# The four mLSTM heads: next head's projections and output gates as chunks inside a head's chain

## The reference

```python
u = rms_norm(x) @ w_in_odd        # q, k, v, o of 4 heads x 256, and input and forget gates
k = k / 16;  o = sigmoid(o)       # per head
# log forget gates summed along the tokens, a running maximum m as stabiliser,
# weights w[t, s] = exp(gate_s - m_t) for s <= t
# prompt:  h = ((q k^T) * w) v / max(|den|, exp(-m)),  den = row sums of (q k^T) * w
# samples: C = decay * C + inp * k v^T,  n likewise,  h = C q / max(|n q|, exp(-m))
y = x + concat_heads(head_norm(h) * o) @ w_out_odd
```

## Time and profile before

| | us |
|---|---|
| median of 3 runs | 3177.26 (3173.38 to 3179.24) |
| the profiled execution | 3176.19 |
| its span, first to last instruction | 3174.5 |
| PE, DVE, ACT busy in the span | 2564.2, 1857.0, 958.3 |
| granted TensorE clock, mean of the span | 0.881 of 2.4 GHz |
| the four heads, first L2382 copy to the last `head_over` | 1550.3 to 1921.0 |

### The profile page before, as it was taken

One profiled execution on the slowest core, in us unless ns is written; L12 is line 12 of the kernel. 1 busy time (PEld: TensorE's weight loads), 2 busy tenths in 40 slices (PEclk: granted clock), 3 DMA queues, 4 the chain that ended last, 5 costly groups with the idle time before them and its releaser, 6 DMA issues. The chain is left out here.

```text
span 3174.5 us, 44526 instructions
## 1 busy us (share of the span) xinstructions
PE 2564.2 (81%) x17937; PEld 1897.6 (60%) x17937; DVE 1857.0 (58%) x2161; ACT 958.3 (30%) x1339; POOL 179.1 (6%) x268
## 2 busy tenths in 40 slices
PE   5967887777867899997877777868569999999992
PEld 4755665276652688885666555744445665665662
DVE  4366785395331545435556654322459989989983
ACT  2102231001220100002221221200258878878861
POOL 1130000310100000000000000000100000000001
PEclk8977888757878899998989888879789999999995
DMA  4564223431505122122122112114279999999973
GB/s 149 139 190 168 87 99 108 133 116 54 212 0 199 67 107 107 72 83 107 57 107 110 57 73 90 54 53 186 71 275 384 388 377 387 385 380 387 386 284 87
DMA packets 156880, 537.70 MB, mean 169 GB/s; under 512 B 15787, under 2 KB 51543, under 8 KB 149057
## 3 DMA queue, kind: packets, MB, share of 16 engines
q1 hardware_dynamic: 122018, 439.46, 36.9%
q0 software_dynamic: 18528, 85.75, 8.0%
q10 hardware_dynamic: 16128, 9.64, 1.1%
HBM read 501.55 MB, written 45.80 MB: 172 GB/s over the span
## 5 line engine op out<-in xcount | busy, mean ns | idle before, releaser
L720 PE MATMUL scalar_unit<-arena,weight_parts 128*128 128x260 bf16 (+1 forms) x4032 | 481.8, 282 | 81.1 <-DVE arena L1807 67.3
L720 PEld LDWEIGHTS scalar_unit<-arena,weight_parts 128*128 128x128 f16 (+1 forms) x4032 | 400.1, 100 | 160.0 <-issue 45.7
L720 PE MATMUL vector_unit<-arena,weight_parts 128*128 128x260 bf16 (+1 forms) x3936 | 451.6, 277 | 40.2 <-DVEq L2216 18.6
L720 PEld LDWEIGHTS vector_unit<-arena,weight_parts 128*128 128x128 f16 (+1 forms) x3936 | 388.8, 99 | 98.2 <-DVEq L2216 18.7
L1282 PE MATMUL vector_unit<-weight_parts,arena 128*128 128x512 bf16 (+3 forms) x1536 | 318.9, 364 | 3.7 <-PE scalar_unit L1244 3.0
L1282 PEld LDWEIGHTS vector_unit<-weight_parts,arena 128*128 128x128 f16 (+1 forms) x1536 | 148.3, 98 | 150.7 <-issue 8.0
L2639 DVE SCALAR_TENSOR_TENSOR weight_parts<-stream_ring,weight_parts 128x2048 f16<-128x2048 f32 (+2 forms) x108 | 204.8, 1940 | 21.6 <-ACT weight_parts L1666 21.3
L2639 DVE SCALAR_TENSOR_TENSOR weight_parts<-arena,weight_parts 128x2048 f16<-128x2048 f32 (+2 forms) x106 | 196.5, 1896 | 27.4 <-ACT weight_parts L1666 27.4
L1756 DVE TENSOR_TENSOR weight_parts<-stream_ring,weight_parts 128x4096 bf16<-128x4096 f32 (+3 forms) x45 | 184.2, 4094 | 1.5
L1666 ACT ACTIVATE weight_parts<-stream_ring 128x2048 bf16<-128x2048 f32 (+2 forms) x108 | 170.6, 1631 | 10.6 <-PE scalar_unit L1282 10.1
L1325 ACT ACTIVATE squares<-residual 128x520 f32<-128x520 f32 x56 | 35.7, 637 | 457.3 <-DVEq L1818 402.3
(11 more groups left out here) (477 smaller groups left out, 3424.0 us busy)
## 6 DMA issues: line engine op xcount, KB each, us to landing
stream_ring<-in_expert_w_gu SPq DMA_DIRECT2D x80, 1024.0 KB, 9.6
arena<-in_expert_w_gu SPq DMA_DIRECT2D x80, 1024.0 KB, 9.3
arena<-in_expert_w_dn SPq DMA_DIRECT2D x64, 704.0 KB, 8.3
stream_ring<-in_expert_w_dn SPq DMA_DIRECT2D x64, 704.0 KB, 8.4
stream_ring<-in_mem_kv SPq DMA_DIRECT2D x16, 2048.0 KB, 7.7
stream_ring<-in_ffn_w_gu SPq DMA_DIRECT2D x11, 2048.0 KB, 7.9
stream_ring<-in_xattn_wkv SPq DMA_DIRECT2D x8, 2048.0 KB, 7.9
stream_ring<-in_w_in_odd SPq DMA_DIRECT2D x8, 2048.0 KB, 8.6
```

Of the source, the lines that this page charges most:

```text
L720: ins = mm(u[0:cols, a * 512:a * 512 + w], weight if i else weight.bitcast(F16), x.bitcast(F16) if j else x, start=(k == 0 and i + j == 0) ...
```

## The change

Queries and keys get two buffers, used by heads in turn (`HQS`, `HKS`). The second pair lies over the first four rows of FM: so the rows that are needed in all heads move to rows 4 and 5, and the samples' gate columns go to a small tile FS. PE gets `head_chunk(c)`, which runs one chunk of 48 matmuls and posts `parts_free` itself after each fourth. Chunks 0 to 5 (q, k, v) of head 0 run before the loop. Inside a head, chunks 6 and 7 (the head's own output gates) stand behind the second and the fourth block of scores; chunks 0 to 5 of the next head stand behind the second key half, the first and the second query half, the sum for the sample denominators, and (two) the sum of squares. ACT reads each of them at matching places: the output gates behind the exponentials, queries and keys behind the state, values behind the square root, and posts `head_ready` after these. DVE splits the load with chunks 0 to 3 of the next head at a head's start and the load with its chunks 4 to 7 behind the gate work, ahead of the copies to HH.

The diff, with renamings and blank lines left out; the remarks behind # are added here:

```diff
-    HQ = at(4160, 2, T)
-    HK = at(5200, 2, T)
+    HQS = [at(4160, 2, T), at(14480, 2, T)]
+    HKS = [at(5200, 2, T), at(15520, 2, T)]
+    FS = at(24040, 2, NB, rows=4)
...
+        def head_chunk(c):
+            if c % 4 == 0:
+                pe.wait_ge(sem("parts_ready"), due("parts_ready"))
+                parts_used[0] += 1
+            wt = parts[:, (parts_used[0] - 1) % 2].rearrange("p t (c k m) -> p t c k m", c=4, k=DC)
+            pe.wait_ge(sem("scalar_unit_free"), due("scalar_unit_free"))
+            u = take_unit["scalar"]()
+            for a in range(2):
+                for k in range(DC):
+                    for i, j in ((0, 0), (0, 1), (1, 0)):
...
+            ins.then_inc(sem("scalar_unit_ready"), 1)
+            if c % 4 == 3:
+                pe.wait_ge(sem("scalar_unit_ready"), due("scalar_unit_free", 0))
+                pe.sem_inc(sem("parts_free"), 1)
+        for c in range(6):
+            head_chunk(c)
         for h in range(NH):
-            project(H, 8, DC, 4, ["scalar"] * 8)
+            HQ, HK, last = HQS[h % 2], HKS[h % 2], h == NH - 1
...
                 ins.then_inc(sem("vector_unit_ready"), 1)      # after a block of scores
+                if sb_ % 2:
+                    head_chunk(6 + sb_ // 2)
...
                     ins.then_inc(sem("vector_unit_ready"), 1)  # after a half of L1178
+                    if not last and (src is HQ or half):
+                        head_chunk(0 if src is HK else 1 + half)
...
             ins.then_inc(sem("vector_unit_ready"), 1)          # after L1185
+            if not last:
+                head_chunk(3)
             pe.wait_ge(sem("head_out"), due("head_out"))
             over_features(sq, 2, "vector")
+            if not last:
+                head_chunk(4)
+                head_chunk(5)
...
+        read_queries(0)
+        read_values()
         for h in range(NH):                                    # ACT
-            if h:
-                act.wait_ge(sem("head_over"), due("head_over"))
-            for i, dst in enumerate((HQ, HK, HV, HO)):
...
             act.wait_ge(sem("w_exp"), sent("w_exp"))
+            if h:
+                act.wait_ge(sem("head_over"), due("head_over"))
+            for c in range(2):
+                read_chunk(HO[:, c, :], ACT.Sigmoid)
             act.wait_ge(sem("c_in"), 16 * (h + 1))
...
                 act.sem_inc(sem("c_prompt_done"), 1)
+            if h + 1 < NH:
+                read_queries(h + 1)
             act.wait_ge(sem("head_h"), due("head_h"))
...
             act.wait_ge(sem("root"), sent("root"))
+            if h + 1 < NH:
+                read_values()
+                act.sem_inc(sem("head_ready"), 1)
...
+        for i in range(2):                                     # DVE, gate part
+            V.tensor_copy(FS[:, i, :], FM[0:4, i, S:T]).then_inc(sem("vector_steps"), 1)
...
         dve.sem_inc(sem("gate_rows"), 1)
+        split_weights()
         for h in range(NH):
-            split_weights()
             split_weights()
...
             dve.wait_ge(sem("w_exp"), due("w_exp"))
+            if h + 1 < NH:
+                split_weights()
             for part in range(2):                              # copies to HH
```

More of the change, by code:

```diff
@@ L1114, in _ @@
         project(H, 1, DC, 1, ["scalar"], cols=64, wait_chunks="normed")
+        def head_chunk(c):
[8 more added lines that the diff above has]
+                    for i, j in ((0, 0), (0, 1), (1, 0)):
+                        weight, x = wt[:, i, c % 4, k, :], H[:, j, k, a * HT:a * HT + HT]
+                        ins = mm(u[:, a * 512:a * 512 + HT], weight if i else weight.bitcast(F16), x.bitcast(F16) if j else x,
+                                 start=(k == 0 and i + j == 0), stop=(k == DC - 1 and i == 1))
+            ins.then_inc(sem("scalar_unit_ready"), 1)
[4 more added lines that the diff above has]
+            head_chunk(c)
         for h in range(NH):
-            project(H, 8, DC, 4, ["scalar"] * 8)
+            HQ, HK, last = HQS[h % 2], HKS[h % 2], h == NH - 1
             if h == 0:
@@ L1134, in _ @@
             u = take_unit["vector"]()
-            mm(u[:, 0:S], pick[:, h, :], FM[0:4, 3, 0:S], start=True, stop=True)
-            mm(u[:, S:S + NB], pick[:, h, :], FM[0:4, 0, S:T], start=True, stop=True)
-            ins = mm(u[:, S + NB:S + 2 * NB], pick[:, h, :], FM[0:4, 1, S:T], start=True, stop=True)
+            mm(u[:, 0:S], pick[:, h, :], FM[0:4, 4, 0:S], start=True, stop=True)
+            mm(u[:, S:S + NB], pick[:, h, :], FS[:, 0, :], start=True, stop=True)
+            ins = mm(u[:, S + NB:S + 2 * NB], pick[:, h, :], FS[:, 1, :], start=True, stop=True)
             ins.then_inc(sem("vector_unit_ready"), 1)
@@ L1581, in _, with read_chunk, read_queries, read_values @@
         act.wait_ge(sem("gate_arg"), due("gate_arg"))
-        A(FM[0:4, 4, :], FM[0:4, 3, :], ACT.Ln).then_inc(sem("gate_value"), 1)
+        A(FM[0:4, 3, :], FM[0:4, 4, :], ACT.Ln).then_inc(sem("gate_value"), 1)
         act.wait_ge(sem("gate_value"), sent("gate_value"))
         act.wait_ge(sem("gate_arg"), due("gate_arg"))
-        A(FM[0:4, 5, 0:S], FM[0:4, 4, 0:S], ACT.Exp, scale=-1.0).then_inc(sem("gate_value"), 1)
+        A(FM[0:4, 5, 0:S], FM[0:4, 3, 0:S], ACT.Exp, scale=-1.0).then_inc(sem("gate_value"), 1)
         act.wait_ge(sem("gate_value"), sent("gate_value"))
-        for h in range(NH):
-            if h:
-                act.wait_ge(sem("head_over"), due("head_over"))
-            for i, dst in enumerate((HQ, HK, HV, HO)):
[L1592 to L1597, removed]
+        def read_chunk(dst, fn=ACT.Copy, factor=1.0):
+            act.wait_ge(sem("scalar_unit_ready"), due("scalar_unit_ready"))
+            u = next_unit()
+            A(split(dst), halves(u), fn, scale=factor).then_inc(sem("scalar_unit_free"), 1)
+            act.wait_ge(sem("scalar_unit_free"), sent("scalar_unit_free"))
+        def read_queries(h):
+            for c in range(2):
+                read_chunk(HQS[h % 2][:, c, :])
+            for c in range(2):
+                read_chunk(HKS[h % 2][:, c, :], factor=0.0625)
+        def read_values():
+            for c in range(2):
+                read_chunk(HV[:, c, :])
+        read_queries(0)
+        read_values()
+        for h in range(NH):
             if h == 0:
@@ L1603, in _ @@
                 act.sem_inc(sem("gc_ready"), 1)
-            act.sem_inc(sem("head_ready"), 1)
+                act.sem_inc(sem("head_ready"), 1)
             for dst in (KTOK, VTK):
@@ L2329, in _ @@
         dve.wait_ge(sem("gates_raw"), due("gates_raw"))
-        ig, lf, e_, u_, l_, x_ = (FM[0:4, i, :] for i in range(6))
+        ig, lf, e_, u_, l_, x_ = (FM[0:4, i, :] for i in (0, 1, 2, 4, 3, 5))
         V.tensor_scalar(u_, lf, -1.0, None, ALU.mult).then_inc(sem("vector_steps"), 1)
@@ L2366, in _ @@
         dve.wait_ge(sem("vector_steps"), sent("vector_steps"))
+        for i in range(2):
+            V.tensor_copy(FS[:, i, :], FM[0:4, i, S:T]).then_inc(sem("vector_steps"), 1)
+            dve.wait_ge(sem("vector_steps"), sent("vector_steps"))
         V.tensor_copy(MMP[0:4, 0:1], l_[:, S - 1:S]).then_inc(sem("vector_steps"), 1)
@@ L2372, in _ @@
         dve.sem_inc(sem("gate_rows"), 1)
+        split_weights()
         for h in range(NH):
-            split_weights()
+            HQ, HK = HQS[h % 2], HKS[h % 2]
             split_weights()
```

## The result

The changed kernel takes 3123.9 us (median of 4 runs, 3119.1 to 3129.9) against 3176.7 for the kernel before on the same chip: a ratio of 0.983, with an interval of 0.982 to 0.985. The forecast was 3122. The profiled execution took 3124.8, its span is 3123.1.

What follows compares the result with a forecast made beforehand. No engine was full: each head ran dense projection chunks, then DVE's chain, in series. Three heads -46.8, entry -10.1 and last head +2.2 gave -54.7 us, from 3177.26 to 3122 us, range 3110 to 3151.

Steps and rivals of the forecast that it cites:

- the last head: Last head: no split and no next head, but chunks 6 and 7 stand in it: 2.2 us more.
- 1, wait for score block 2 (L2452): Scores: chunk 6 stands ahead of score block 2, ready at tau 8.85 where DVE wanted it at 7.73: +1.2 us.
- step 2: Weight split moved into mid-chain, ahead of DVE copies that the third product needs: +5.9 us, including the scores' 1.2.
- 3, waits for the query halves: States: the next head's chunks 0 and 1 delay the two query halves: +2.45 and +2.35 us.
- step 4: Norm: chunk 3 and ACT's read stand before the squares, +3.6 us; sums take 1.9 instead of 3.42, -1.5.
- step 5: To the next head: DVE's other split comes last, next copy at tau 84.4; PE's work has 3.9 us of cover.
- The clock: Lower clock after two PE pauses of over 3 us, before the third product and score block 1: 2 us a head.
- Rival (a): Clock falls at both pauses, slowing the whole f32 block and chunk 6: 11.5 us a head, 3151 us; chance 0.20.
- The sentence on the Trainium skill: Bursts after pauses start cold, transposes don't count as activity: chunk 6 cold in every head, 3131 us; possible only.
- The entry: Before the first chain: six chunks stand there instead of eight, 10.1 us less.
- (b): Chunks stay at the half clock, cut up by waits: a head about 140 us, the kernel 3290 us; chance 0.05.
- (c): Chunk 3 or 5 waits for a split held up behind DVE's chain: heads near 102 us, kernel 3167 to 3177; chance 0.05.

Runs made afterwards that it cites:

- e1: Changed kernel with the mid-chain weight split moved to where DVE waits for the sums of squares: 3103.4 us, 0.978 of the kernel before.
- e3: Changed kernel with the next head's chunks 0 to 3 put back behind the chain, after the sums of squares: 3158.6 us, 0.994 of the kernel before.
- e6: Changed kernel with ACT's squares put ahead of its read of chunk 3: 3122.9 us, 0.983 of the kernel before.
- e2: Changed kernel with the mid-chain split moved to DVE's wait for the sums, and the head-start split put in mid-chain: 3114.2 us, 0.981 of the kernel before.
- e5: Changed kernel with 12 unused f32 matmuls filling each of PE's two pauses of over 3 us: 3117.6 us, 0.981 of the kernel before.
- e8: Changed kernel with the mid-chain split moved to DVE's wait for the sums, and the head-start split in three pieces in the chain: 3102.1 us, 0.976 of before.
- e4: Changed kernel with chunks 6 and 7 (output gates) put back ahead of the chain: 3156.0 us, 0.994 of the kernel before.

## Why the prediction was right

The sum for the stage was -54.7 and the stage fell by 54.7, but two errors cancel: the three heads gave 48.0 instead of 46.8, and the last head lost 3.5 instead of 2.2. That the total agrees to a tenth is luck; the terms agree to about 1.3. By step, for head 1, in tau from the copy at 1633.01:

| step | predicted | measured |
|---|---|---|
| 1, wait for score block 2 (L2452) | 1.2 | 1.1 (2.8 in the last head, behind a slow chunk 6) |
| 2, split in mid-chain | 15.1 to 21.9 | 15.0 to 21.7 |
| 2, L2489 | 25.05 | 26.8 |
| 3, L2520 | 33.3 | 35.1 |
| 3, waits for the query halves | 2.45, 2.35 | 2.39, 2.09 |
| 4, sums of squares | 1.9 long | 2.02 long |
| 4, L2565 | 65.7 | 66.8 |
| 5, PE's row ready | 80.5 | 81.5 |
| 5, next copy | 84.4, with the clock 86.4 | 85.7 |

**Steps 1 to 5** hold in kind, and but for the clock to about 0.4 us in size; e1 (step 2), e3 (steps 3 and 4), e6 (step 4) and e2 (step 5) each undid one, and each moved the stage the way of its step. The 1.75 us by which L2489 is late is the clock: the third product takes 4.11 us, and 2.42 in e5. Some of it is made up again further on, for L2565 is only 1.1 late. In step 4, e6 puts the read ahead of the squares at 1.8 us.

**The clock** was put at 2 us a head outside the steps, for either of two pauses. Both pauses stood where the prediction had them (3.28 us before the third product, 3.17 before the score block), and e5 prices them at 1.1 to 1.7 a head. So this term was about 0.6 too large, which covers the 0.4 a head that came beyond the forecast. Rival (a) had the clock fall at both pauses and take the f32 block with it; in the kernel after only one is hit in a head, and behind the third product the f32 block is back at its pace (1.12 and 3.72 us for row and state in head 1). As its sign the prediction named a granted clock of 1.00 around tau 20 to 30 and at chunk 6, and 0.5 as that of (a). By this sign the forecast did not come out clean: the clock is 0.57 at the third product of head 1 and 0.70 and 0.86 at the score block and chunk 6 of head 2. What sets it apart from (a) is the size, 1.4 us a head by e5 against 11.5.

The sentence on the Trainium skill (TensorE: Matmul & The Clock Gate, section HAM oscillation, and Part 4) would have chunk 6 cold, at the lower clock, in every head. Head 0 has no pause ahead of its chunk 6 (5.48 us). In heads 1 to 3, with the same transposes and the same 3.17 us pause ahead of it, chunk 6 takes 5.48, 7.10 and 6.78 us: in one of three it isn't cold, and in the other two it loses 1.6 and 1.3 us and not the 4.9 that the prediction charged. So here the measurement decides against the rule as the prediction applied it.

**The last head** is the term that was mis-sized: +2.2 forecast, +3.5 measured. The prediction charged the clock to three heads only, but the fourth copy has the same pause behind it. These are the score block and chunk 6 of the last head of after:

```profile
1805.30 1.98 PE L1166 MATMUL vector_unit<-arena 128*128 128x384 f32 x4 [3.17 <-DVE arena L2437]
1807.07 6.78 PE L1128 MATMUL scalar_unit<-arena,weight_parts 128*128 128x260 bf16 x48
```

Chunk 6 is 1.3 us longer there than at the full clock, and e5's last head is 1.3 us shorter than that of after.

**The entry** was 10.18 us shorter, against 10.1. Rivals (b) and (c) left no trace: a chunk in the chain spends 5.32 us from start to start at the full clock, and in head 1 of after no chunk waits for a late split.

**What stays open.** Why the clock falls at the first pause in heads 0 and 1 and at the second in heads 2 and 3 (in heads 1 and 2 of e6 at both) isn't settled; e5 only shows that it falls at neither when they are filled. Nor was the cause found of the several us ahead of the stage. They begin early: a norm's first step at 247.8 us in the profile of before stands at 250.5 in that of after, at 246.2 in e1 and at 252.8 in e8, in work that no edit touches.

## What to carry to other kernels

Work that is moved into a chain of waits should be laid against each engine's queue in order: four chunks of PE hid 21 us of its work for some 7 us of delay in the chain (e3), while one weight split on DVE, moved ahead of work that PE waited for, cost about 4 us a head until it went to a place where DVE waits anyway (e1), or was cut so that a short copy could pass between its pieces (e8). Price dense filler for two things, its own time and the clock that it keeps up for the sparse work behind it. Count a pause in every pass of the loop, the last one too.

## What the runs showed of the hardware

- Dense chunks inside a sparse chain held the clock: with chunks 6 and 7 ahead of them the two first products take 4.55 us after a pause of 0.30 (after), without them 6.27 after one of 3.10 (e4).
- Of two pauses of nearly the same length (3.28 and 3.17 us) only one was followed by the lower clock in heads 1 and 2 of after, the first in head 1 and the second in head 2; e3 took a pause of 3.27 before the third product at no loss in head 1 (2.42 us). A pause of 2.09 us ahead of the sums of squares was followed by it in head 0 of e1 and e5 and in head 2 of e8 (sums 2.55, 2.61 and 3.00 us), and not in the other inner heads of these runs (2.02 us).
- A small saving can be lost to the clock: e6 cut a wait by 1.8 us a head, and over half of it came back in slower matmuls in that run.
